# A two-block transformer kernel on one core: the roots of five RMS norms applied behind the matrix products, the rotary tables made on GpSimd, and the first attention head's start rearranged

## What is computed

```python
h = rms_norm(x, attn_norm[0]);  x = x + diff_attention(h, ...)        # 8 heads, rotary, q/k norms
x = x + swiglu(rms_norm(x, ffn_norm[0]), w_gate_up[0], w_down[0])      # hidden 2816
kw, vw = shared_kv(x, cos, sin, kv_norm, w_kv, k_norm)
h = rms_norm(x, attn_norm[1]);  x = x + swa_sink_attention(h, ...)     # window 128, sinks
x = x + swiglu(rms_norm(x, ffn_norm[1]), w_gate_up[1], w_down[1])
```

## Time and profile before

| | us |
|---|---|
| median of 3 runs (3073.27 to 3077.53) | 3075.73 |
| profiled execution, its own time | 3078.21 |
| its span in the trace | 3076.3 |
| PE busy | 2794.8 (91%) |
| DVE busy | 1682.3 (55%) |
| ACT busy | 1269.5 (41%) |
| POOL busy | 639.8 (21%) |

### The profile page before, as it was taken

The page is one execution under the profiler, slowest core; times in us unless marked ns, Lnnn a source line. Parts: engine busy times, 40 slices in busy tenths (PEclk is TensorE's granted clock), DMA queues, the critical chain, the costliest instruction groups (busy, mean ns, idle before and its releaser), DMA issues.

```text
span 3076.3 us, 41620 instructions
## 1 busy us (share of the span) xinstructions
PE 2794.8 (91%) x14244; PEld 2339.8 (76%) x14244; DVE 1682.3 (55%) x2544; ACT 1269.5 (41%) x2121; POOL 639.8 (21%) x298
## 2 busy tenths in 40 slices
PE   4989899998687899997987899999997899899998
PEld 4777687886576778886875788888886887688886
DVE  5776534445665443435996465254455455464645
ACT  3444365654366365654211233132233466352422
POOL 0111077874011087873000000000000000000000
PEclk9999899998799999998997899999998999999999
DMA  3111244543100245443110111122111000222221
GB/s 122 42 44 60 82 157 158 177 157 117 42 19 25 82 171 175 163 162 103 55 52 31 55 55 61 56 69 69 61 36 55 28 29 8 69 89 89 96 94 63
DMA packets 67905, 252.07 MB, mean 82 GB/s; under 512 B 7456, under 2 KB 8736, under 8 KB 64928
## 3 DMA queue, kind: packets, MB, share of 16 engines
q1 hardware_dynamic: 67744, 249.99, 23.8%
HBM read 247.87 MB, written 2.10 MB: 81 GB/s over the span
## 4 chain that ended last, share of the span: by engine, by line
PE 45%; issue 21%; DVE 19%; POOL 7%; ACT 5%; DVEq 2%; ACTq 1%; DMA 0%; POOLq 0%
PE psum L1680 11%; PE psum L1681 11%; PE psum L1679 11%; POOL mod_p L485 7%; DVE work L1203 4%; DVE w_lo L1079 2%; PE psum L2035 2%; DVE work L1308 1%; ACT work L870 1%; ACT w_hi L568 1%; PE psum L1818 1%; DVE hx_lo L1302 1%; ACT sw_pt L882 1%; PE psum L1689 1%; PE psum L1796 1%
## 5 line engine op out<-in xcount | busy, mean ns | idle before, releaser
L1079 DVE TENSOR_TENSOR w_lo<-w_raw,w_hi 128x1024 fp32r<-128x1024 f32 (+3 forms) x334 | 447.8, 1341 | 415.8 <-ACT w_hi L568 403.5
L1679 PE MATMUL psum<-hx_hi,w_hi 128*128 128x512 f32 x1568 | 623.6, 398 | 29.6 <-DVE w_lo L1079 14.3
L1680 PE MATMUL psum<-hx_lo,w_hi 128*128 128x512 f32 x1568 | 625.1, 399 | 0.0
L1681 PE MATMUL psum<-hx_hi,w_lo 128*128 128x512 f32 x1568 | 623.7, 398 | 0.0
L485 POOL TENSOR_TENSOR mod_p<-mod_w,mod_c 128x1024 f32<-128x1024 f32 x192 | 547.6, 2882 | 186.7 <-ACT mod_p L553 150.8
L568 ACT ACTIVATE w_hi<-w_raw 128x1024 fp32r<-128x1024 f32 (+3 forms) x334 | 356.3, 1067 | 271.3 <-PE psum L1681 214.9
L475 POOL TENSOR_TENSOR tok_r<-tok_ms,half 128x4 f32<-128x4 f32 (+1 forms) x70 | 71.8, 1026 | 1857.7 <-DVE tok_ms L1003 1245.2
L1679 PEld LDWEIGHTS psum<-hx_hi,w_hi 128*128 128x128 f32 x1568 | 297.0, 189 | 80.6 <-issue 16.6
L1681 PEld LDWEIGHTS psum<-hx_hi,w_lo 128*128 128x128 f32 x1568 | 296.9, 189 | 70.4
L1680 PEld LDWEIGHTS psum<-hx_lo,w_hi 128*128 128x128 f32 x1568 | 297.6, 190 | 48.8
L1679 PE MATMUL psum<-a_hi,w_hi 128*128 128x512 f32 (+1 forms) x656 | 233.9, 357 | 19.4 <-DVE a_lo L1144 10.6
(11 more groups left out here) (263 smaller groups left out, 4954.4 us busy)
## 6 DMA issues: line engine op xcount, KB each, us to landing
mod_w<-in_w_mod SPq DMA_DIRECT2D x96, 512.0 KB, 3.6
w_raw<-in_fup SPq DMA_DIRECT2D x88, 512.0 KB, 4.6
w_raw<-in_cup SPq DMA_DIRECT2D x88, 512.0 KB, 3.5
w_raw<-in_fdown SPq DMA_DIRECT2D x32, 512.0 KB, 4.6
w_raw<-in_cdown SPq DMA_DIRECT2D x32, 512.0 KB, 3.5
w_raw<-in_da_qkv SPq DMA_DIRECT2D x8, 1536.0 KB, 6.4
w_raw<-in_fdown SPq DMA_DIRECT2D x16, 384.0 KB, 4.6
w_raw<-in_cdown SPq DMA_DIRECT2D x16, 384.0 KB, 3.0
```

Of the source, the lines that this page charges most:

```text
L1079: dve.tensor_tensor(w_lo[:, off:off + n], w_raw[:, raw:raw + n], w_hi[:, off:off + n].bitcast(F32), ALU.subtract).then_inc(s_lo, 1)
L1679: pe.matmul(dst, wh, xh, start=first, stop=False)
L1680: pe.matmul(dst, wh, xl, start=False, stop=False)
L1681: return pe.matmul(dst, wl, xh, start=False, stop=last)
```

## The change

- Five norms are `late`: attn_norm0, ffn_norm0, kv_norm, attn_norm1 and ffn_norm1. The product runs on `X` times gain, without the root. Of ffn_norm0 and ffn_norm1 the gain comes with the rounding: in the last `resid`, ACT writes `hx_hi` beside the square, and DVE `hx_lo` one block later (`feed`). For kv and q, `X` goes in as it is (`feed="none"`), and the gains are multiplied into the weights, in 8 pieces of 256 columns where one instruction split 2048 columns (`wgain`). For the first head the gain comes with the rounding.
- The roots are applied as ACT's scale, one number per partition, where the head, k, v and q projections are evacuated. In the ffn up stages, where tokens lie along the row, ACT copies the spread root to SBUF once (`root_b`), and it is multiplied in on DVE: a gate block is multiplied out of PSUM before the SiLU, which now works in SBUF, and the SiLU's result is multiplied once more before it meets the value block. A 1-element clear behind the first of these tells ACT.
- PE sums the squares and spreads the root behind the 6th and 8th input tile of the first pair of the ffn; in `kv`, behind the first projection.
- At the start, positions and rows are loaded first, then `X` and the first head's weights tile by tile; POOL computes the angles (23 instructions on 128x128 or less) and the head tables (19); PE runs head 0's projections for all four token tiles input tile by input tile, as they arrive; the second head's weights are loaded in two DMAs into a buffer of their own, and two of its projections are done before the first slot, whose slots 0 and 1 then leave theirs out. Sine and cosine stay on ACT.
- Sums of squares use a two-step instruction (times 1.0, plus) where they used a plain addition.

The core of the diff:

```diff
+    add("resid", KT_D, k=KT_D, toks=SEQ, w="da_wo", src="O", gates=None, squares=SEQ, ready=7, feed="ffn_norm0")
+    norm(toks=SEQ, late=True, spread=True)
+    ffn("ffn", 0, SEQ, "f", SEQ, feed="none")
+    norm(toks=SEQ, late=True)
+    add("kv", 2, w="sw_kv", tag="a", ctx=False, wgain="kv_norm")
+    add("q", 4, w="sw_q", tag="a", ctx=False, wgain="attn_norm1")
+    add("resid", KT_D, k=KT_D, toks=SEQ, w="sw_wo", src="O", gates=None, squares=SEQ, feed="ffn_norm1")
...
+            sp.dma_start(pos_i[:], dram["pos"]).then_inc(s_small, 16)
+            sp.dma_start(row[:], dram["row"]).then_inc(s_small, 16)
+            sp.dma_start(vec[:, 0:KT_D], dram["vec"][:, 0:KT_D]).then_inc(s_gain, 16)
+            for k in range(KT_D):
+                sp.dma_start(X[:, k, 0:SEQ], dram["x"][:, k, :]).then_inc(s_xk[k], 16)
+                sp.dma_start(w_raw[:, 384 * k:384 * (k + 1)], dram["da_qkv"][0, :, 384 * k:384 * (k + 1)])\
+                    .then_inc(s_first[k] if k < 2 else s_xk[k], 16)
+            sp.dma_start(vec[:, KT_D:], dram["vec"][:, KT_D:]).then_inc(s_in, 16)
             sp.dma_start(ident[:], dram["ident"]).then_inc(s_in, 16)
             sp.dma_start(masks[:], dram["masks"]).then_inc(s_in, 16)
             sp.dma_start(axial[:], dram["axial"]).then_inc(s_in, 16)
+            for c in (slice(0, 3 * D // 2), slice(3 * D // 2, 3 * D)):
+                sp.dma_start(second_raw[:, c], dram["da_qkv"][1, :, c]).then_inc(s_loaded[0], 16)
...
+                for period in (2 * math.pi * 4096, 2 * math.pi):
+                    pool.tensor_scalar(turns, ang, 1.0 / period, ROUND, ALU.mult, ALU.add)
+                    pool.drain()
+                    pool.tensor_scalar(turns, turns, ROUND, None, ALU.subtract)
+                    pool.drain()
+                    for part in trig_split(period):
+                        pool.tensor_scalar(trig_t, turns, -part, None, ALU.mult)
+                        pool.drain()
+                        pool.tensor_tensor(ang, trig_t, ang, ALU.add)
+                        pool.drain()
+                pool.tensor_scalar(turns, ang, -3.1415925, 3.1415925, ALU.max, ALU.min)
...
+                for t in range(4):
+                    cos = trig[:, 0, t, :].unsqueeze(1).broadcast_to([P, 4, 32])
+                    sin = trig[:, 1, t, :].unsqueeze(1).broadcast_to([P, 4, 32])
+                    tc = da_tab_c[:, t].rearrange("p n (h f) -> p n h f", h=2)
+                    ts = da_tab_s[:, t].rearrange("p n (h f) -> p n h f", h=2)
+                    pool.tensor_tensor(tc[:, :, 0, :], g[:, :, 0, :], cos, ALU.mult)
+                    pool.tensor_tensor(tc[:, :, 1, :], g[:, :, 1, :], cos, ALU.mult)
+                    pool.tensor_tensor(ts[:, :, 0, :], second_neg, sin, ALU.mult)
+                    pool.tensor_tensor(ts[:, :, 1, :], g[:, :, 0, :], sin, ALU.mult).then_inc(s_tabs, 1)
+                    pool.drain()
...
+            angles()
+            head_tables()
...
+            act.wait_ge(s_gain, 16)
+            for k in range(KT_D):
+                act.wait_ge(s_xk[k], 16 if k < 2 else 32)
+                act.activation(hx_hi[:, k, :], X[:, k, 0:SEQ], ACT.Copy, scale=vcol("attn_norm0", k)).then_inc(s_hhi, 1)
+                if k < 2:
+                    act.wait_ge(s_first[k], 16)
+                cols = slice(384 * k, 384 * (k + 1))
+                act.activation(w_hi[:, cols], w_raw[:, cols], ACT.Copy).then_inc(s_whi0 if k < KT_D - 1 else s_hi, 1)
+                if k >= 3:
+                    act.wait_ge(s_acc, k - 1 if k > 3 else 2)
+                act.activation(wk[:, SQ_SLOT[k % 3], 0:SEQ], X[:, k, 0:SEQ], ACT.Square).then_inc(s_sq, 1)
+                act.drain()
+                if k == 5:
+                    sines()
+            act.wait_ge(s_loaded[0], 32)
+            for part in range(3):
+                act.activation(w_hi[:, 3 * D + D * part:4 * D + D * part], second_raw[:, D * part:D * part + D], ACT.Copy)\
...
+                if st["kind"] == "ffn" and st.get("late"):
+                    act.wait_ge(s_rb, st["late"]["norm0"] + 1)
+                    act.activation(root_b[:], ps_lin(3, 0, SEQ), ACT.Copy).then_inc(s_rbs, 1)
...
+                    if st["feed"]:
+                        gain = vcol(st["feed"], b) if st["feed"] != "none" else 1.0
+                        act.activation(hx_hi[:, b, :], X[:, b, 0:n], ACT.Copy, scale=gain).then_inc(s_hhi, 1)
...
-                        act.wait_ge(s_mm, b + (st["block0"] + 1))
-                        act.wait_ge(s_a, q + (st["tile0"] + 1))
-                        act.activation(wk[:, s // 2, 0:toks], ps_of(st, s, 0, toks), ACT.Silu).then_inc(s_gate, 1)
+                        act.wait_ge(s_gsc, q + (st["gate0"] + 1))
+                        act.activation(wk[:, s // 2, 0:toks], wk[:, s // 2, 0:toks], ACT.Silu).then_inc(s_gate, 1)
                         act.drain()
...
+                    act.activation(da_qk[:, t, :], pb[:, bank, 0:256], ACT.Copy, scale=root)
...
+            def low_weights(st, off, raw, k):
+
+                cols = slice(off + 256 * k, off + 256 * (k + 1))
+                return dve.scalar_tensor_tensor(w_lo[:, cols], w_raw[:, raw + 256 * k:raw + 256 * (k + 1)],
+                                                vcol(st["wgain"], k), w_hi[:, cols].bitcast(F32), ALU.mult, ALU.subtract)
...
+                def feed(b):
+                    dve.wait_ge(s_hhi, st["feed0"] + b + 1)
+                    hi = hx_hi[:, b, :].bitcast(F32)
+                    if st["feed"] == "none":
+                        r = dve.tensor_tensor(hx_lo[:, b, :], X[:, b, 0:SEQ], hi, ALU.subtract)
+                    else:
+                        r = dve.scalar_tensor_tensor(hx_lo[:, b, :], X[:, b, 0:SEQ], vcol(st["feed"], b), hi,
+                                                     ALU.mult, ALU.subtract)
+                    r.then_inc(s_h, 1)
+                    dve.drain()
+                    add_square(b, b)
...
+                        dve.wait_ge(s_mm, b + (st["block0"] + 1))
+                        dve.wait_ge(s_rbs, st["layer"] + 1)
+                        dve.tensor_tensor(gate, ps_of(st, s, 0, toks), root_b[:], ALU.mult).then_inc(s_ev, 1)
+                        dve.drain()
+                        dve.memset(ratio[:, 3:4], 0.0).then_inc(s_gsc, 1)
                         return
-                    q = 2 * i + s // 2
+                    dve.wait_ge(s_gate, q + (st["gate0"] + 1))
+                    dve.scalar_tensor_tensor(gate, gate, 1.0, root_b[:], ALU.mult, ALU.mult)
+                    dve.drain()
                     dve.wait_ge(s_mm, b + (st["block0"] + 1))
-                    dve.wait_ge(s_gate, q + (st["gate0"] + 1))
-                    dve.tensor_tensor(wk[:, 2 + s // 2, 0:toks], ps_of(st, s, 0, toks), wk[:, s // 2, 0:toks],
-                                      ALU.mult).then_inc(s_ev, 2)
+                    dve.tensor_tensor(wk[:, 2 + s // 2, 0:toks], ps_of(st, s, 0, toks), gate, ALU.mult).then_inc(s_ev, 1)
                     dve.drain()
                     low_part(q, wk[:, 2 + s // 2, 0:toks], toks, q + (st["tile0"] + 1), hi=o_hi, lo=o_lo)
...
+                if st["src"] == "H" and st.get("late"):
+                    pair(st, 0, 6)
+                    sum_squares(st["late"])
+                    pair(st, 6, 8)
+                    spread_roots(st["late"])
+                else:
+                    pair(st, st.get("ready", 0), st["k"])
...
+                for k in range(KT_D):
+                    pe.wait_ge(s_h, k + 1)
+                    if k < KT_D - 1:
+                        pe.wait_ge(s_wlo0, k + 1)
+                    else:
+                        pe.wait_ge(s_lo, 1)
+                    wh, wl = w_hi[:, 384 * k:384 * (k + 1)], w_lo[:, 384 * k:384 * (k + 1)]
+                    for t in range(4):
+                        xh, xl = h_tile(k, t)
+                        dst = pb[:, t, 0:384]
+                        pe.matmul(dst, xh, wh, start=k == 0, stop=False)
+                        pe.matmul(dst, xh, wl, start=False, stop=False)
+                        r = pe.matmul(dst, xl, wh, start=False, stop=k == KT_D - 1)
+                        if k == KT_D - 1:
+                            r.then_inc(S["pj"], 1)
+                            if t == 1:
+                                sum_squares(stages[0])
+                pe.wait_ge(S["pje"], 1)
+                project(4, 0, 1, 1)
+                pe.wait_ge(s_in, 16 * LOADS_IN)
+                turn_qk(0, 0)
+                pe.wait_ge(S["pje"], 2)
+                project(5, 1, 1, 1)
+                turn_qk(1, 1)
+                turn_qk(2, 2)
+                pe.wait_ge(S["pje"], 4)
+                pe.wait_ge(s_constb, 1)
                 for i in range(4):
                     slot(0, 0, i, first=True)
                 with pe.Fori(0, 2) as p:
```

(24 more changed lines are left out.)

344 lines of the change are left out of this document (202 added, 142 removed).

## The result

| | before | after |
|---|---|---|
| median, us | 3075.7 (3073.3 to 3077.5) | 3194.9 (3190.5 to 3201.0) |
| profiled execution, its own time, us | 3078.2 | 3196.0 |
| its span, us | 3076.3 | 3194.1 |
| mean granted PE clock | 0.953 | 0.940 |

What follows compares the result with a forecast made beforehand. PE was not alone: in the ffns the ACT, DVE and POOL round (21.6 us) nearly matched PE's 22.5; at norms PE stood. 3078.2 - 17 - 20 - 26 + 100 = 3115, median 3113; range 3060 to 3145.

Steps and rivals of the forecast that it cites:

- The ffns' round: Group of four ffn blocks on ACT, DVE, POOL: grows from 21.6 to 27.3 us, above PE's 22.5; about 100 us lost.
- the norms' gain: Norms before the two ffns: PE's stand and clock loss go, 8.4 us in the first, 17 for both.
- the rescale at 1.1 us: Odd ffn positions: SiLU result times root before the product, 0.69 to 0.95 plus 0.25 gap; 2.2 us a group.
- the place in line: Even ffn positions: SiLU waits for DVE's weight split, multiplication and clear; 0.85 + 2.6 us a group.
- the prediction's own stage-by-stage sum: Each ffn: 14, 8 and 4 us in the up parts, 8, 8, 7 at down stages; about 50 us.
- the count of leads: In the ffns: PE at most three blocks ahead; one block's lead off part one, 11 us off parts two and three.
- Rival C: Ffns: added rescales and splits wait half a 2.88 us POOL product, 1.4 us, twice more a group; 3163, chance 0.07.
- the rescale at over 2 us in the mean: Ffns, trace of after: L1079 and the rescale at over 2 us in the mean would show the port-contention rival.
- The start: Kernel start: first scores at 45.5 instead of 70.03, slots shorter by a net further 1.5; gain 26 us, bounds 12 and 30.
- rival B: Start gives little: POOL's instructions at 0.9 us make tables and root late, 14 of 26 us gone; 3127, chance 0.08.
- The slots: Slots 0 and 1 lose a 4 us projection each, but DVE needs nearly the whole slot: 1.5 us more gain.
- kv and q: Kv starts 13 us earlier, q gains 9 less 1 for clock, weight pieces cost 3.6; gain 20, bounds 16 and 23.

Runs made afterwards that it cites:

- the kernel with the gate in PSUM: After, with SiLU's result written back to PSUM and both added gate multiplications reading PSUM ahead of weight splits; 3038.0 us, ratio 0.987.

## Why the prediction was wrong

**Direction and mechanism held.** The ffns' round of ACT, DVE and POOL was the thing to look at, it outgrew PE's 22.5 us, PE waits for `w_lo` in stands of 9 us or so ahead of the down stages, and the norms' gain is 9.4 and 7.5 us, 16.9 against 17.

**The step that failed is the rescale at 1.1 us**, priced from L1157's 0.69 and L1144's 0.95. It took 2.65 with a gap of 0.17, 1.7 us more, twice a group: 27.3 + 3.4 = 30.7, and the measured round is 30.0, since the place in line was dearer in my sum (3.4) than it is (2.4). Put the 30.0, a step of 7.5, into the prediction's own stage-by-stage sum: 4 by 7.5 less 5.6 is 24, 30 less 11 is 19, 3 by 7.5 less 11 is 11.5, and the starts of the down stages are 9.4, 9.4 and some 8.4 (measured 9.7, 9.6 and 9.1). That is 82 us in each ffn instead of 49, and twice the difference of 33 is the 66 us by which the ffns passed the forecast. So the one duration carries the error. That it comes out so evenly is luck in part: the trace has 78.5 and 76.3 for these stages, of which 4.8 and 3.9 are clock losses in the inner down stages, so the count of leads was 8 to 10 us too high in each ffn; and in and behind the last down stages 6.6 and 4.9 us were lost, where the sum had little.

**Why the rows misled.** L1144's 0.95 and the split's 1.55 are not a surcharge of 0.26 for two inputs in SBUF. Each of these started when a product was nearly over and waited for what was left of it. GpSimd in the kernel before, four products one after the other:

```profile
400.30 11.52 POOL L485 TENSOR_TENSOR mod_p<-mod_w,mod_c 128x1024 f32<-128x1024 f32 x4 [0.99 <-ACT mod_p L553]
```

The fourth ends at 411.82, and L1144 at 411.42 + 0.95 = 412.37, 0.55 behind it; the first, 2.37 long, ends at 402.67, and the split at 403.80, 1.13 behind it. The 2.88 of the earlier trace rows is a price of that kind too: with VectorE's turn in it, while a product alone takes 2.37. I read the price of a fortunate moment as the price of the operation. Rival C had the right mechanism, but with a mean wait of half a product and a chance of 0.07; its sign, the rescale at over 2 us in the mean, came, though the split stayed under it. The meeting is no matter of chance: ScalarE's sum (L648) releases GpSimd's pair, the same engine then copies the weights, that releases the split, and behind it comes the rescale, 3.3 to 3.7 us after the pair began, every time 0.2 to 0.3 us into the second product (417.36 against 419.46 - 2.37 = 417.09). C's 3163 was still 32 short: it counted 62 us of waits in all, and the rescales alone lost 44 by 1.96 = 86.

The rule of the Trainium skill (SBUF — State Buffer, Who interferes with whom) was the better guide than my row: the pair of ports is held for a whole instruction, and the other engine waits. The traces agree: 0.69 without products, 1.54 with half products, 2.65 with whole ones, and 0.69 always with one input in PSUM.

**The start** gave 17.8 us, not 26. The sums' means were ready at 28.8, near enough (27.5 + 1.5), but GpSimd's tables stood ahead of the root. Timelines of after:

```profile
28.80 0.16 DVE L1119 TENSOR_SCALAR tok_ms<-psum 128x4 f32<-128x4 f32 x1 [1.15 <-PE psum L1865]
29.05 4.24 DVE L1162 TENSOR_TENSOR w_lo<-second_raw,w_hi 128x1024 fp32r<-128x1024 f32 x3
...
30.78 1.43 POOL L550 TENSOR_TENSOR da_tab_s<-work,trig 128x128 f32<-128x128 f32 x1
...
34.39 0.45 POOL L550 TENSOR_TENSOR da_tab_s<-work,trig 128x128 f32<-128x128 f32 x1
34.99 1.04 POOL L502 TENSOR_TENSOR tok_r<-tok_ms,half 128x4 f32<-128x4 f32 x1 [0.16 <-issue]
...
49.55 0.49 PE L1990 MATMUL psum<-da_T 64*128 64x128 f32 x2 [0.49 <-ACT da_v L842]
```

The 42 instructions end at 34.8, started at 4.4: 0.72 us each with gaps, between the 0.45 that I took and rival B's 0.9. One product of the tables takes 0.45 us behind VectorE's split of the second head's weights and up to 1.43 during it, so part of this price looks like the same contention; that was not tried apart. (Two sums of the prediction don't add up here: 27.5 + 1.5 + 0.3 + 1.0 is 30.3, not 31, and 5 + 10 + 2 + 8 is 25, not 27.) B's mechanism came half true, 6 us late, and scores at 49.6 instead of 45.5. The slots then cost 2.7 where I had 1.5 (0.2 to 2.7 in the kernels that share this code).

**kv and q** gave 18.2 us, close to 20; but the attention behind them got 4.3 us longer in after, and 2.6 to 3.4 longer in the variants, which I had at nothing. The scaled evacuation of 256 columns takes ScalarE 0.47 us instead of 0.38, and PE's waits for ScalarE's `sw_sq` went from 8.3 to 14.1 us over the kernel. That this is the cause was not tried. In the kernel with the gate in PSUM the stretch from the last down stage to the window attention's scores is 116.2 us against 129.0 (16.4 less behind PE's last matmul, 3.6 more in the down stage, which now feeds the next product), and with the attention the gain is 9.5. So 10 of the 17 us by which that kernel missed its 3021 are this term.

**The sum by terms:** -17.8 (26 forecast) - 16.9 (17) - 18.2 + 4.3 (20) + 85.1 + 81.2 (50 each) + 0.2 = +118, the difference of the two spans. Of the 81 us between 118 and the forecast's 37, 66 are the ffns, 8 the start, 6 kv and q with the attention behind them.

## What to carry to other kernels

A duration under contention is a row plus a moment: before taking it as a price, see where in the other engine's instruction it began, and whether the new instruction will fall on the same phase every time. On VectorE, beside GpSimd, count the inputs that lie in SBUF: an operand left in PSUM kept an added instruction at 0.69 us where two in SBUF cost 2.65, and that, with a place in the line where the engine waited anyway, turned a loss of 119 us into a gain of 38. Where that can't be had, shorter instructions on GpSimd shorten the wait.

## What the hardware showed that I had not expected

- VectorE and GpSimd alternate by whole instructions when VectorE's instruction has both inputs in SBUF and GpSimd multiplies there: from the end of the running product VectorE's instruction needs 0.55 us for 512 columns and 1.08 for 1024, and a pair of products of 2.37 us each takes 5.73 with VectorE beside it. The form, two-step or plain, makes no difference (2.645 and 2.644 us).
- After a stand of 9.7 us PE runs at 1.2 GHz for some 4.6 us (granted clock 0.54 from 470 to 475 us, 1.00 behind it). In the four inner down stages, in which PE never waits, such a start cost 1.5 to 2.7 us each.
- ScalarE can write a result back into a PSUM bank at 0.60 us for 512 columns, where writing to SBUF took 0.64, so that PSUM serves as a second scratch space out of GpSimd's way.
